# Dilated attention with tokens sorted into even and odd, paired heads, and split tensors placed at 2048-byte steps

## What is computed

```python
DIL_PATTERNS = ((128, 1), (512, 4), (2048, 16))      # window, dilation
for gi, (window, dilation) in enumerate(DIL_PATTERNS):
    o_g, lse_g = dilated_group_attention(dq[:, :, gi], dk[:, :, gi], dv[:, :, gi], slopes[gi],
                                         dilation, window // dilation)
alpha = jax.nn.softmax(jnp.stack(lses, axis=0), axis=0)
o_c = jnp.sum(alpha[..., None] * jnp.stack(outs, axis=0), axis=0)
```

## Time and profile before

| | |
|---|---|
| median of 3 runs | 1424.36 us (1424.35 to 1427.46) |
| time of the profiled execution | 1422.21 us |
| its span, first to last instruction | 1420.4 us |
| TensorE busy | 1382.9 us, 97% |
| DVE busy | 882.9 us, 62% |
| ACT busy | 707.6 us, 50% |
| mean granted TensorE clock | 0.998 of full speed (2.4 GHz) |

### The profile page before, as it was taken

The page is one execution under the profiler, slowest core; times in us unless marked ns, Lnnn a source line. Parts: engine busy times, 40 slices in busy tenths (PEclk is TensorE's granted clock), DMA queues, the critical chain, the costliest instruction groups (busy, mean ns, idle before and its releaser), DMA issues.

```text
span 1420.4 us, 17888 instructions
## 1 busy us (share of the span) xinstructions
PE 1382.9 (97%) x7200; PEld 1159.4 (82%) x7200; DVE 882.9 (62%) x1048; ACT 707.6 (50%) x974; POOL 85.0 (6%) x77
## 2 busy tenths in 40 slices
PE   8999999999999999999999999999989999999998
PEld 5788878987877888878878998777878789987777
DVE  6656556648877655556774565547667655664475
ACT  5544445568545544446755444434457554444442
POOL 0000000000001000001440000000013500000000
PEclk9999999999999999999999999999999999999999
DMA  7866636524467766635644434534456544344442
GB/s 257 272 209 199 202 120 212 169 63 133 146 199 233 224 187 185 189 118 169 210 147 148 136 118 143 154 120 135 153 193 193 175 146 122 119 133 146 121 132 76
DMA packets 63706, 231.00 MB, mean 163 GB/s; under 512 B 7446, under 2 KB 7574, under 8 KB 63496
## 3 DMA queue, kind: packets, MB, share of 16 engines
q1 hardware_dynamic: 61632, 223.90, 50.3%
q10 hardware_dynamic: 1992, 5.97, 1.3%
HBM read 228.79 MB, written 1.05 MB: 162 GB/s over the span
## 4 chain that ended last, share of the span: by engine, by line
PE 76%; DVE 12%; ACT 4%; POOL 3%; DMA 3%; issue 2%; SPq 0%; ACTq 0%; POOLq 0%; DVEq 0%
PE psum L1766 63%; PE psum L1810 4%; PE psum L1948 4%; PE psum L1965 3%; POOL rstd L504 3%; DVE w_lo L1089 3%; DMA raw<-weights 2%; DVE y_lo L1089 2%; ACT w_hi L559 1%; DVE squares L1529 1%; POOL mean L500 1%; DVE arena L1383 1%; PE psum L2212 1%; DVE norm L1127 1%; DVE arena L1574 1%
## 5 line engine op out<-in xcount | busy, mean ns | idle before, releaser
L1089 DVE TENSOR_TENSOR w_lo<-raw,w_hi 128x1024 fp32r<-128x1024 f32 x226 | 275.1, 1223 | 165.7 <-ACT w_hi L559 163.0
L559 ACT ACTIVATE w_hi<-raw 128x1024 fp32r<-128x1024 f32 x226 | 237.6, 1055 | 166.0 <-PE psum L1766 150.2
L1766 PE MATMUL psum<-w_hi,x_hi 128*128 128x512 f32 (+1 forms) x584 | 234.0, 401 | 4.0 <-DVE x_lo L1135 2.5
L1089 DVE TENSOR_TENSOR y_lo<-raw,y_hi 128x1024 fp32r<-128x1024 f32 x144 | 175.1, 1221 | 93.0 <-ACT y_hi L559 92.2
L1766 PE MATMUL psum<-w_hi,x_lo 128*128 128x512 f32 (+1 forms) x584 | 227.8, 390 | 0.0
L1766 PE MATMUL psum<-w_lo,x_hi 128*128 128x512 f32 (+1 forms) x584 | 227.6, 390 | 0.0
L559 ACT ACTIVATE y_hi<-raw 128x1024 fp32r<-128x1024 f32 x144 | 151.5, 1055 | 108.6 <-PE psum L1766 90.4
L1766 PE MATMUL psum<-y_hi,x_hi 128*128 128x512 f32 (+1 forms) x408 | 163.1, 400 | 0.1
L1766 PE MATMUL psum<-y_hi,x_lo 128*128 128x512 f32 (+1 forms) x408 | 159.3, 391 | 0.0
L1766 PE MATMUL psum<-y_lo,x_hi 128*128 128x512 f32 (+1 forms) x408 | 159.2, 390 | 0.0
L1766 PEld LDWEIGHTS psum<-w_hi,x_hi 128*128 128x128 f32 x584 | 110.1, 189 | 33.6 <-issue 9.2
(11 more groups left out here) (190 smaller groups left out, 2382.0 us busy)
## 6 DMA issues: line engine op xcount, KB each, us to landing
raw<-weights SPq DMA_DIRECT2D x422, 512.0 KB, 4.0
arena<-gains ACTq DMA_DIRECT2D x7, 512.0 KB, 4.6
res<-x SPq DMA_DIRECT2D x2, 512.0 KB, 5.4
arena<-lru_w ACTq DMA_DIRECT2D x1, 1024.0 KB, 5.0
cst<-consts ACTq DMA_DIRECT2D x1, 736.0 KB
arena<-gains SPq DMA_DIRECT2D x1, 512.0 KB, 5.0
out<-res SPq DMA_DIRECT2D x1, 512.0 KB, 2.6
out<-res SPq DMA_DIRECT2D x2, 256.0 KB, 2.0
```

The lines of the kernel that those rows point to most:

```text
L559: act.activation(slot(t)[0], raw[:, t % RAW, :], ACT.Copy).then_inc(hi_ready, 1)
L1089: dve.tensor_tensor(lo, raw[:, t % RAW, :], hi.bitcast(F32), ALU.subtract).then_inc(lo_ready, 1)
L1766: ins = pe.matmul(out_, a, b, start=start and n == 0, stop=stop and n == 2, skip_group_check=skip)
```

## The change

It has six parts.

1. `DIL_UNITS`: 8 units instead of 12 in a layer, each with one query tile and two neighbouring heads h and h + 1. Tokens are sorted: tile 0 of the dilated attention holds the even tokens, tile 1 the odd ones. Dilations 4 and 16 link only tokens of the same parity, so their keys are those of the own tile (128); dilation 1 takes all 256. A unit has 2 score products of 256 columns and 4 of 128, issued head by head in turn (rows 0 to 63, rows 64 to 127), into a PSUM bank per head; 16 value products and 8 transposes.
2. The sorting: `dil_copy` reads each transposed block from PSUM with a step of 2, as 4 instructions of 256 columns in place of 1 of 1024; the values come sorted out of `dense_strided` (chunks 7, 8, 9), where the stationary columns of x are taken with a step of 2; so does the c_z gate (chunk 11). The heads are sorted back when y2 is split after `turn_heads`, with outputs at a step of 2 (4 instructions on ACT and 4 on DVE in place of 2 and 2).
3. With 11 units in all, the last unit's values come in chunk 20, `turn_heads` in chunk 21, and m = 0, 1, 2 hold no attention.
4. Block 1's scores are issued even and odd in turn.
5. w, x, y1, y2 start at a multiple of 2048 (`ROW`), and so does tail.
6. DVE's order: `dil_sum` comes one `refill` earlier in chunks 4 to 7; from layer 0 to layer 1 the second `res` addition (and, on ACT, `pre_square(4 + l, 1)`) comes ahead of the splits of five weight tiles.

```diff
-DIL_UNITS = [(0, [h, h + 2]) for h in (0, 1, 4, 5)] + [(1, [h]) for h in range(DIL_HEADS)]
+DIL_UNITS = [(qt, [h, h + 1]) for qt in range(TOK) for h in range(0, DIL_HEADS, 2)]
...
-        w_hi = sb("w_hi", [P, BASE_SLOTS, TILE], F32R)
+        w_hi = sb("w_hi", [P, BASE_SLOTS, TILE], F32R, ROW)
...
-        tail_at = arena_at + 4 * FFN_TAIL
+        tail_at = -(-(arena_at + 4 * FFN_TAIL) // ROW) * ROW
...
+        def strided(v):
+            return v.rearrange("p (a r) -> p r a", r=STRIDE)
+        def grouped(v):
+            return v.rearrange("p (r a) -> p r a", r=STRIDE)
...
-                    act.activation(dst[:, 4 * g:4 * g + 4, :].rearrange("p f s -> p (f s)"), wide(4, 1024), ACT.Copy,
-                                   scale=gain).then_inc(dil_copied, 1)
+                    for f in range(4):
+                        ins = act.activation(grouped(dst[:, 4 * g + f, :]), strided(turned[:, f * SEQ:(f + 1) * SEQ]),
+                                             ACT.Copy, scale=gain)
...
+            def dense_strided(t, q, out_):
+                pe.wait_ge(lo_ready, t + 1)
+                for tok in range(TOK):
+                    for j, k in enumerate((2 * q, 2 * q + 1)):
+                        lh = [strided(v[:, k, :])[:, tok, :]
+                              for v in (x_hi, x_lo)]
+                        rh = [w[:, 512 * j:512 * (j + 1)] for w in slot(t)]
+                        ins = three(out_[:, tok, :], lh, rh, k == 0, k == KD - 1)
...
-                    scores(u, [(q_rows(h, qt), k_rows(h, width)) for h in heads], width)
+                    half = len(heads) // 2
+                    order = [n + half * b for n in range(half) for b in range(2)]
...
+                    for g, lo, hi, keys in ((0, 0, 256, slice(0, SEQ)), (1, 256, 384, own), (2, 384, 512, own)):
+                        for n, h in enumerate(heads):
+                            r = slice(HEAD * n, HEAD * (n + 1))
+                            items.append((psum[:, 4 + n, lo:hi], dil_q[r, 4 * g + h // 2, own],
+                                          dil_k[r, 4 * g + h // 2, keys]))
...
+                        if c == 21 and q == 1:
+                            turn_heads(At(4, l, 2))
```

More of the change, by code:

```diff
@@ L40 @@
 TAIL_SLOTS = 4
+ROW = 2048
 FFN_TAIL = 12864
@@ L1019, in _ @@
                                            ).then_inc(mla_copied, 1)
-                    if c == 23:
-                        probs_copy(At(UB + UNITS_LAYER, l, UNITS_LAYER))
                     refill(t + 3)
+                    if c == 21:
+                        act.wait_ge(heads_turned, At(4, l, 2))
+                        turned = wide(4, 1024)
+                        for f in range(4):
+                            ins = act.activation(strided(y2_hi[:, f, :]), grouped(turned[:, f * SEQ:(f + 1) * SEQ]),
+                                                 ACT.Copy, scale=0.5)
+                            if f % 2:
+                                ins.then_inc(heads_hi, 1)
                     if c == 8:
@@ L1675, in _ @@
                         add_product(c - 22, 0)
-                    if c == 23:
-                        last_values()
                     refill(t + 3)
+                    if c == 21:
+                        turned = wide(4, 1024)
+                        for f in range(4):
+                            if f % 2 == 0:
+                                dve.wait_ge(heads_hi, At(6 + f // 2 + 1, l, 4))
+                            ins = rest(strided(y2_lo[:, f, :]), grouped(turned[:, f * SEQ:(f + 1) * SEQ]), 0.5,
+                                       strided(y2_hi[:, f, :]))
+                            if f % 2:
+                                ins.then_inc(heads_lo, 1)
                     if c == 2:
@@ L1943, in fill_ready, with scores @@
                     pe.wait_ge(*freed(fill - 2, l))
-            def scores(u, items, width):
-                for n, (q_, k_) in enumerate(items):
-                    ins = pe.matmul(wide(4, 1024)[:, n * width:(n + 1) * width], q_, k_, start=True, stop=True)
+            def scores(u, items):
+                for out_, q_, k_ in items:
+                    ins = pe.matmul(out_, q_, k_, start=True, stop=True)
                 ins.then_inc(scores_ready, 1)
@@ L2070, in unit_scores @@
                         pe.wait_ge(k_copied, 1)
-                    scores(u, [(q_rows(h, qt), k_rows(h, width)) for h in heads], width)
+                    half = len(heads) // 2
+                    order = [n + half * b for n in range(half) for b in range(2)]
+                    scores(u, [(wide(4, 1024)[:, n * width:(n + 1) * width], q_rows(heads[n], qt),
+                                k_rows(heads[n], width)) for n in order])
                 for q in range(4):
@@ L2398, in constants @@
     c[:, C_MASK2:C_MASK2 + SEQ] = np.where(back >= 0, 0.0, NEG)
-    for g, dil in enumerate(DILATIONS):
-        ok = (back >= 0) & (back % dil == 0) & (back <= dil * DIL_BACK)
-        c[:, C_DIL + g * SEQ:C_DIL + (g + 1) * SEQ] = np.where(ok, back, BIG)
+    place = np.arange(SEQ)
+    token = STRIDE * (place % (SEQ // STRIDE)) + place // (SEQ // STRIDE)
+    tiles = [(0, 0, place), (0, 1, place), (1, 0, place[:P]), (2, 0, place[:P])]
+    at = C_DIL
+    for g, qt, keys in tiles:
+        dist = token[qt * P:(qt + 1) * P, None] - token[keys][None, :]
+        ok = (dist >= 0) & (dist % DILATIONS[g] == 0) & (dist <= DILATIONS[g] * DIL_BACK)
+        c[:, at:at + len(keys)] = np.where(ok, dist, BIG)
+        at += len(keys)
     for at, half in ((C_ROPE1, HALF), (C_ROPE2, ROPE2 // 2)):
```

117 lines of the change are left out of this document (52 added, 65 removed).

## The result

The changed kernel takes 1382.14 us (median of 4 runs, 1381.03 to 1382.54) against 1424.36: a ratio of 0.9696, with a 95% interval of 0.9682 to 0.9710, 42.2 us less. The prediction was 1325, 99 us less. What came is rival A (1380); through it alone the stated range, 1314 to 1386, holds the result. The profiled execution took 1382.27 us, 39.9 less than that of before.

The account below looks back on a forecast made before the run. TensorE's own list was taken as the bound (1382.9 of 1420.4 us busy). From the profiled 1422.2, 40.0 for the edits and 59.4 for starts gave 1322.8, plus 2.1 for the runs: 1325 us, range 1314 to 1386.

Parts of the forecast that it names:

- rival A: Split products: the 13 ns extra is fixed, only tail gains, 3.9 us, so 1380 us; chance 0.27.
- Starts at 2048: Split products: aligned starts remove the 13 or 20 ns extra; 63.4 us, 59.4 after what is given back.
- Scores, 18.6 and 1.1: Score products pair across row halves: 18.6 us saved in the layers' dilated units, 1.1 in block 1.
- Rival D: Dilated scores: products of alternating halves don't run side by side, 1.97 us a unit, 1342 us in all; chance 0.07.
- Values, transposes, getting in and out, behind transposes, behind `turn_heads`: TensorE: fewer value products 3.6 us, transposes 1.7, unit entries and exits 1.5; waits gone behind transposes 3.0, `turn_heads` 3.9.
- `turn_dil`, 4.6: TensorE's waits for the dilated scaling shrink as the sum comes earlier: 4.6 us, between 2.3 and 6.4.
- Layer step, 2.0: Between the layers: `turn_norm`'s 3.04 us wait goes, 1 given back; 2.0 us saved, between 0 and 3.
- Stationary operands with a step of 2, nothing: 384 products: the 0.189 us weight load stays hidden beneath a 0.227 us step, so no cost.
- Rival C: Weight loads with a step of 2 outlast the products: 82 us more, 1407 us or slower; chance 0.05.
- Copies with a step of 2, nothing: ACT's `dil_copy`: 4 copies of 0.48 us in place of 1, below 2 us a chunk, costing nothing.
- the case of doubled copies: ACT's `dil_copy`: if a step of 2 doubled the copies, to 3.8 us, it would cost 1.1 us a layer.

Follow-up runs that it names:

- run 4: The kernel before with only the starts at multiples of 2048 (tail too) changed: 1422.7 us, ratio 0.9975 to the kernel before.
- run 1: Small separate kernel of 24 equal products, varying operand starts, stationary step and columns, width and type: 512 columns took 0.2267 us at best in float32r, 0.2163 in bf16.
- run 3: Small separate kernel varying width and type, starts at multiples of 2048: float32r 0.148 us for 320 columns, 0.2025 for 448; bf16 0.056 for 128.
- run 5: The changed kernel with all tensors back at their old starts, tail at 832 again: 1385.45 us, ratio 0.9717 to the kernel before.
- run 7: The changed kernel with dilated score products issued head by head and block 1's in the old order: 1390.97 us, ratio 0.9759 to the kernel before.
- run 8: The changed kernel with dil_sum back behind its split in chunks 4 to 7: 1389.58 us, ratio 0.9754 to the kernel before.
- run 11: The changed kernel with the old order on ScalarE and VectorE at the step from layer 0 to 1: 1383.96 us, ratio 0.9715 to the kernel before.
- run 12: The changed kernel again, unaltered, on the same chip as the run with the old layer-step order: 1381.33 us, ratio 0.9702 to the kernel before.
- run 6: The changed kernel with stationary columns of x at a step of 1 in chunks 7, 8, 9, 11 (output differs): 1379.54 us, ratio 0.9682.
- run 9: The changed kernel with the first half of the third gated addition on VectorE two splits earlier: 1376.58 us, ratio 0.9660 to the kernel before.

## Why the prediction was wrong

- **Starts at 2048: the step that failed.** "I read it as a partly used first piece of 256 bytes that costs as if it were whole." Of 63.4 us gained at this step, 59.4 after what is given back, 3.9 came by the steps (3.2 to 3.6 by the time of run 4). The two extras, 13 and 20 ns, aren't one thing: 13 ns are there in float32r at every start and in bf16 at none (runs 1 and 3), and 7 ns came from tail's distance to the stationary operand within 256 bytes (runs 1, 4 and 5). That 128 and 192 bytes fitted both "with nothing left over" was chance. The rows of before could have warned me: two points can't test a rule made from them, and no streamed operand of a split product started on a multiple of 256 there. Rival A was right in both parts.
- **Scores, 18.6 and 1.1.** Right: 1.08 us a unit (1.09 forecast), 1.09 in block 1 (277.76 - 276.67 in the trace; 1.11 forecast), and by run 7 the alternation carries it. Rival D, that they don't pair, is refuted; run 7 lies between D and the forecast.
- **Values, transposes, getting in and out, behind transposes, behind `turn_heads`.** The counts are as forecast and the waits are missing from the trace; these terms, 13.7 us together, were not tried one by one.
- **`turn_dil`, 4.6.** Mis-sized on the low side: 5.9 of wait in the trace, 7.4 by run 8.
- **Layer step, 2.0.** 2.6 by the medians of runs 11 and 12, within the 0 to 3; their intervals overlap.
- **Stationary operands with a step of 2, nothing.** Mis-sized: 2.5 us, 384 products of 6.6 ns (run 6). A load of 0.189 us beneath a step of 0.227 is not free on that ground alone. Rival C, 82 us, is refuted.
- **Copies with a step of 2, nothing.** Right. ACT's 256-column copies lasted 474 ns each against 478 contiguous, so the case of doubled copies, 1.1 us a layer, did not come:

```profile
L950 ACT ACTIVATE arena<-psum,arena 128x256 f32<-128x256 f32 x48 | 18.8, 474 | 21.8 <-PE psum L1844 21.8
```

- **A wait that I didn't look for.** With attention and `turn_heads` out of m = 0 to 2, TensorE reaches `turn_merged(0)` sooner while VectorE still has three splits ahead of the addition. In the profile it costs 2 x 1.9 us of wait and 2 x 1.6 us of half clock; run 9 gives 5.6 for it.

Sum in the profile: rival A's 43.9 less 2.5 (step of 2), less 3.0 (the waits at `turn_merged(0)`, 2 x 1.9 us, of which before had 2 x 0.4), less 3.1 (slow products) plus 1.0 (before's own, behind the 3.04 us wait), plus 1.3 (`turn_dil`) is 37.6; 39.9 were measured. 2.3 us are not itemised. That the result lies so near rival A's 1380 is in part luck: of the costs that the prediction left out (2.5 + 3.0 + 3.1 = 8.6 us), about half were made up by 1.0, 1.3 and the 2.3 that are not itemised.

What stays open is where float32r's 11 ns over bf16 come from: they were there at every start, at every width from 256 columns up, and with fewer stationary columns.

## What to carry to other kernels

Before a per-product extra is read as a matter of place, measure it in a small kernel that varies the start alone: two sizes that fit a rule don't make it one. Place the two operands of a float32r product with their starts equal modulo 256 bytes, and count 3 to 7 ns for each 512-column product whose starts are not, or 7 for one whose stationary operand has a step of 2. When work is taken out of a stretch of the bounding engine, look for the next value that another engine must deliver there, and move its step ahead of splits that have time.

## What the runs showed of the hardware that I had not expected

- A float32r product took 0.2267 us for 512 columns at best, bf16 0.216. The extra over 0.2133 is 13 ns against 2.5.
- Of the operands' places, the distance between the two starts is what counts (0.2267 to 0.228 at a multiple of 256 bytes, 0.2296 at 64, 0.2329 at 128, 0.2333 at 192), and a stationary step of 8 adds 18 ns.
- Products in opposite row halves pair when they alternate (1.08 us for 12 records, 1.09 by the sum for full pairing), and only partly when each half comes in one piece (1.61).
- An idle of 1.9 us of TensorE was followed by 4 to 8 products at 1.2 GHz in 7 of 14 cases, and not in the other 7, at the same two places of the program.
